# HGRN2 attention stage: first level's exponents made in the projection's last two blocks, output product's weights asked for behind the last level's products

## The reference, cut to what matters

```python
def hgrn2_chunk_scan(q, k, v, log_f):          # chunks of C = 128 tokens, two of them; 8 heads of 128
    def step(state, inp):
        qi, ki, vi, gi = inp
        b = jnp.cumsum(gi, axis=-2)
        rel = b[..., :, None, :] - b[..., None, :, :]
        decay = jnp.exp(jnp.where(lower, rel, -jnp.inf))
        attn = jnp.sum((qi[..., :, None, :] * ki[..., None, :, :]) * decay, axis=-1)
        o_intra = jnp.einsum('bhts,bhsv->bhtv', attn, vi)
        o_inter = jnp.einsum('bhtd,bhdv->bhtv', qi * jnp.exp(b), state)
        ...

def hgrn2_mixer(h, w_in, lb, norm_g, w_out):
    proj = h @ w_in                            # q, forward f, backward f, values, output gate
    ...
    o = rms_norm(o_fw + o_bw, norm_g) * jax.nn.silu(g)      # a scan forward and one backward
    return o @ w_out
```

## Time and profile before

| | us |
|---|---|
| median of 3 runs | 2471.93 (2466.46 to 2472.8) |
| the profiled execution, its own time | 2469.02 |
| its span, first to last instruction | 2467.3 |
| projection's last blocks, attention, next stage's start | 500 to 540.1, 540.1 to 608.1, from 608.1 |

### The profile page before, as it was taken

One profiled execution on the slowest core, in us unless ns is written; L12 is line 12 of the kernel. 1 busy time (PEld: TensorE's weight loads), 2 busy tenths in 40 slices (PEclk: granted clock), 3 DMA queues, 4 the chain that ended last, 5 costly groups with the idle time before them and its releaser, 6 DMA issues. The chain is left out here.

```text
span 2467.3 us, 46378 instructions
## 1 busy us (share of the span) xinstructions
PE 2294.8 (93%) x15836; PEld 1997.5 (81%) x15836; DVE 1769.4 (72%) x3162; ACT 1233.7 (50%) x1967; POOL 311.4 (13%) x289
## 2 busy tenths in 40 slices
PE   7979988987999999998999998699999999899997
PEld 7647756963699999996888887579999999788886
DVE  5764774766458887886776768466888888666776
ACT  4543543555444456554445444634446555444544
POOL 0000000000000000003443430100000000333442
PEclk9989999998999999998999999899999999999999
DMA  7554554756247776656777785234776664877775
GB/s 206 193 205 119 184 216 138 264 214 263 98 144 225 231 215 211 185 180 194 242 239 241 242 249 202 102 120 157 227 226 219 198 187 149 258 242 241 239 243 164
DMA packets 247734, 497.92 MB, mean 202 GB/s; under 512 B 58040, under 2 KB 134072, under 8 KB 244304
## 3 DMA queue, kind: packets, MB, share of 16 engines
q1 hardware_dynamic: 247632, 496.55, 62.8%
HBM read 461.82 MB, written 34.65 MB: 201 GB/s over the span
## 5 line engine op out<-in xcount | busy, mean ns | idle before, releaser
L2651 PE MATMUL psum<-split_operands 128*128 128x512 f32 x3072 | 701.0, 391 | 20.5 <-ACT split_operands L2630 20.5
L2651 PEld LDWEIGHTS psum<-split_operands 128*128 128x128 f32 x3072 | 579.3, 189 | 141.7 <-ACT split_operands L2630 20.8
L2389 PE MATMUL psum<-split_operands 128*128 128x256 f32 x4096 | 542.6, 285 | 8.9 <-ACT split_operands L2423 8.8
L2389 PEld LDWEIGHTS psum<-split_operands 128*128 128x128 f32 x4096 | 509.6, 192 | 10.4 <-ACT split_operands L2423 10.4
L2615 POOL TENSOR_TENSOR arena<-arena,residual_gates 128x256 f32 (+1 forms) x256 | 287.9, 1124 | 1644.9 <-DMA residual_gates<-expert_activations 1644.9
L2642 DVE TENSOR_TENSOR split_operands<-weights_ring,split_operands 128x1024 fp32r<-128x1024 f32 x256 | 315.3, 1232 | 201.3 <-ACT split_operands L2630 201.3
L2630 ACT CAST split_operands<-weights_ring 128x1024 fp32r<-128x1024 f32 x256 | 269.5, 1053 | 348.0 <-PE psum L2651 346.4
L2466 DVE TENSOR_TENSOR split_operands<-weights_ring,split_operands 128x1024 fp32r<-128x1024 f32 x256 | 313.1, 1224 | 101.6 <-ACT split_operands L2423 100.8
L325 PE MATMUL psum<-split_operands 128*128 128x256 f32 x2496 | 308.9, 285 | 8.0 <-DVE split_operands L341 5.5
L325 PEld LDWEIGHTS psum<-split_operands 128*128 128x128 f32 x2496 | 303.7, 193 | 15.1 <-DVE split_operands L341 8.5
L2393 PE MATMUL psum<-split_operands 128*128 128x256 f32 x2048 | 288.4, 284 | 0.0
(11 more groups left out here) (320 smaller groups left out, 2025.4 us busy)
## 6 DMA issues: line engine op xcount, KB each, us to landing
weights_ring<-in_peer_u_dram SPq DMA_DIRECT2D x256, 512.0 KB, 3.6
weights_ring<-in_peer_v_dram SPq DMA_DIRECT2D x256, 512.0 KB, 4.3
expert_activations<-residual_gates SPq DMA_DIRECT2D x256, 128.0 KB, 1.8
residual_gates<-expert_activations SPq DMA_DIRECT2D x256, 128.0 KB, 4.0
split_words<-in_w_ada_dram SPq DMA_DIRECT2D x20, 768.0 KB, 6.6
weights_ring<-in_w_in_dram SPq DMA_DIRECT2D x6, 2048.0 KB, 8.5
weights_ring<-in_hg_w_in_dram SPq DMA_DIRECT2D x5, 2048.0 KB, 8.2
arena<-in_hg_w_in_dram SPq DMA_DIRECT2D x5, 2048.0 KB, 8.0
```

Of the source, the lines that this page charges most:

```text
L2389: nc.tensor.matmul(K.ps[:, 4 + b, 0:SEQ], u_t[:, b, 0, k], h[:, wh, k], start=(k == 0 and wh == 0), stop=False)
L2651: return K.nc.tensor.matmul(K.ps[:, 4 + 2 * t + half], g[:, s, w, t * P:(t + 1) * P], vs[:, s % 2, wv, half * 512:(half + 1) * 512], start ...
```

## The change

Unit 0's exponents leave the attention stage. The buffers are now laid out in `hg_memory`, at the same addresses, and the four instructions are issued by VectorE in the projection, one at each of four places behind `FACTORS`. The counts of the semaphores `exps_k` and `exps_q` fall by one, and ScalarE waits for nothing ahead of its first exponential. The helper `level_exponent` holds what `exponents` held. SP's wait ahead of the output product's weights is now for the products of all eight units (`scored`).

```diff
+FIRST_EXPONENTS = [(8, 5), (8, 7), (9, 1), (9, 3)]
+FACTOR_BUFFERS = 3
...
+def level_exponent(K, H, pair, L, i):
+    def halves(a):
+        return a.rearrange("p n (b s j) -> p n b s j", s=2, j=L)
+
+    kf, kb = (H.k[:, d].rearrange("p h c t -> p (h c) t") for d in range(2))
+    ek, eq = (halves(pair[:, w].rearrange("p (n t) -> p n t", t=P)) for w in range(2))
+    middle_f, middle_b = (halves(H.pre[:, d, :, 0:P])[:, :, :, 1, 0:1].broadcast_to([P, HG * CH, P // (2 * L), L])
+                          for d in range(2))
+    out, a, b, op = (
+        (ek[:, :, :, 0], middle_f, halves(kf)[:, :, :, 0], ALU.add),
+        (ek[:, :, :, 1], halves(kb)[:, :, :, 1], middle_b, ALU.subtract),
+        (eq[:, :, :, 1], halves(H.pre[:, 0, :, 1:])[:, :, :, 1], middle_f, ALU.subtract),
+        (eq[:, :, :, 0], middle_b, halves(H.pre[:, 1, :, 0:P])[:, :, :, 0], ALU.subtract))[i]
+    return K.nc.vector.tensor_tensor(out, a, b, op)
...
+        elif (n, k) in FIRST_EXPONENTS:
+            i = FIRST_EXPONENTS.index((n, k))
+            level_exponent(self.K, H, H.factors[:, 0], UNITS[0], i)
...
+    H.factors = area.take(FACTOR_BUFFERS, 2, HG * CH * P)
+    H.factors_end = area.at
...
-            exponents(0)
             for n in range(NU):
                 if n + 1 < NU:
                     exponents(n + 1)
...
         @block.sync
         def _(sp):
             mod.load(sp, 2, 16)
-            sp.wait_ge(exps_q, NU)
+            sp.wait_ge(scored, NU)
...
             for n, L in enumerate(UNITS):
-                act.wait_ge(exps_k, n + 1)
+                if n >= 1:
+                    act.wait_ge(exps_k, n)
...
-                act.wait_ge(exps_q, n + 1)
+                if n >= 1:
+                    act.wait_ge(exps_q, n)
```

More of the change, by code:

```diff
@@ L1491, in stage_hg_attention @@
     nc = K.nc
-    BUFS = 3
+    BUFS = FACTOR_BUFFERS
     NU = len(UNITS)
     with S.open() as (block, sem):
-        area = Area(K.arena, H.end)
-        kq = area.take(BUFS, 2, HG * CH * P)
+        kq = H.factors
+        area = Area(K.arena, H.factors_end)
         exps_k, exps_q, exp_done, pair_ready = sem("exps_k"), sem("exps_q"), sem("exp_done"), sem("pair_ready")
@@ L1501, in stage_hg_attention @@
         q = H.q.rearrange("p h c t -> p (h c) t")
-        kf, kb = (H.k[:, d].rearrange("p h c t -> p (h c) t") for d in range(2))
-        pf, pb = H.pre[:, 0], H.pre[:, 1]
         pre = H.pre.rearrange("p d (h c) t -> p d h c t", c=CH)
@@ L1511, in crossing @@
             return kq[:, n % BUFS, w].rearrange("p (h c t) -> p h c t", h=HG, c=CH)
[L1513 to L1518, removed]
         def last_sum(d):
@@ L1538, in exponents @@
                     return
[L1539 to L1546, removed]
+                level_exponent(K, H, kq[:, n % BUFS], L, 0)
+                level_exponent(K, H, kq[:, n % BUFS], L, 1).then_inc(exps_k, 1)
+                level_exponent(K, H, kq[:, n % BUFS], L, 2)
+                level_exponent(K, H, kq[:, n % BUFS], L, 3).then_inc(exps_q, 1)
             def factors(n):
```

## The result

The changed kernel takes 2474.56 us (median of 17 runs, 2469.68 to 2478.33), the kernel before 2471.01 in as many (2466.46 to 2476.5). The ratio is 1.0013, with a 95% interval of 1.0007 to 1.0019: 3.5 us slower, between 1.7 and 4.7. It moved the way that was forecast, and by less: the forecast was 6.4. It is also less than the 0.3% that the prediction takes as the least change it can tell.

A forecast was written before the change was run, and what follows sets the result against it. VectorE paced most of the attention stage, TensorE's instruction supply its end. Terms 0 + 4.3 + 2.1 = 6.4 us over 2469.02 gave 2475.4, forecast as a 2476.5 median; range 2469.5 to 2483, 8 in 10.

The forecast's parts named there:

- Part 1: First exponents moved from attention to projection: VectorE's list 4.0 us earlier in attention, 0 us added in the projection.
- Rival C: Projection: the four added VectorE instructions aren't covered, 4.6 us on top of the forecast, 2480; chance 0.03.
- T: End of the last unit's products in attention, when the 4 MB of weights are requested: 598.5, between 594.1 and 600.3.
- rival A: Attention, TensorE: instruction lots arrive in time without bulk transfer, stops vanish, T = 594.1, 2472 as a median; chance 0.16.
- B: Attention, TensorE: instruction lots come no faster than before, T = 600.3, +8.7 us, 2479 as a median; chance 0.26.
- The end of the stage: Attention's end: SP's landing is last, next stage begins at T + 13.9 = 612.4 against 608.1, 4.3 us later.
- Rival D: Attention's end: the stores land without waiting for the weights, TensorE ends the stage, 2462 to 2465; chance 0.06.
- The clock: Next stage's first 24 TensorE records: low clock after 10.2 us idle costs 1.4 to 2.6 us more, 2.1 taken.
- the forecast (+3 to +7.4): Whole kernel: the band around the forecast of 6.4 us slower, given chance 0.46.
- Part 2: SP's request for 4 MB of weights moved from 589.47 to T, with four stores and their landing queued behind it.

The follow-up runs named there:

- part 1 alone: Changed kernel with SP's wait for the output product's weights put back to the last query exponents, first exponents still in the projection: ratio 0.9982 to before.
- part 2 alone: Kernel before with only SP's wait ahead of the weights changed to the last products, all exponents in the attention stage: ratio 1.0033 to before.
- stores first: Changed kernel with the stores of the modulation's row issued and waited for ahead of the 4 MB of weights: ratio 0.9971 to before.

## Why the prediction was right, and where a size was off

**Part 1** went as told: the first product of factors was predicted 5.1 us into the stage, and is there at 5.0. In the projection nothing was lost: the stage takes 169.3 in after and 168.2 in before, but 168.2 in part 1 alone and 169.3 in part 2 alone, so the difference isn't the added work's. Rival C falls.

**T** is the term that was mis-sized. I put the last products at 598.5, which is 58.35 from the stage's start, and they ended at 54.85: the first lot of instructions was there 2.1 us sooner (3.2 us behind unit 6's 15th record, where I had taken 5.2), and the second came 3.8 us after the first, where I had again taken 5.2. I had read 5.2 off the stop at 566.16 as the nearest row without the 4 MB, but there the modulation's weights were in transfer. Without a bulk transfer (a DMA share of 0.02) a lot takes 3.6 to 3.8 us, in the six kernels that show both stops, the changed one among them; with the 4 MB 6.3, in two. The packet of instructions itself shows what the transfer adds. In the changed kernel it is transferred at 597.7, 1.2 us behind the first record of the lot before, and TensorE goes on 2.6 us later. This is the DMA in 597.7 to 597.9:

```profile
q8 instruction: 1, 0.02, 41.6%
```

In the kernel before it is transferred at 601.5, 3.8 us behind that record (597.72), and TensorE goes on 2.5 us later (604.02). So the weights hold up the packet's start, and not what follows it. That answers rivals A and B, which stood on either side: the time of a lot is partly its own (A is wrong, 2.2 us of stop remain, though its T of 54.0 was nearer than mine) and partly the transfer's (B is wrong). The Trainium skill, "Runtime: NRT & Kernel Launch", section on instruction fetch mechanics, has the crossing mostly hidden. Here it isn't even on a quiet DMA: 127 records pass in 1.54 us, and a stop of 2.17 follows.

**The end of the stage** followed T as forecast: SP was last, 13.7 us from request to branch (13.3 forecast), the stores behind the weights. Rival D had the stores land apart from them. It falls by SP's wait of 11.4 us, which is 6.7 with half of the weights ahead and 0.9 with none, and by stores first. The stage grew by 1.2 and not by 4.3: T took off 3.5, and the landing added 0.4.

**The clock** had the right mechanism: L1725's 24 records took 7.39 in place of 5.70, 1.7 us more (2.1 forecast). Of the 3.5 to 5.9 us at the low clock that I took, 5.9 stands in a row and 3.5 in none; 4.1 were measured. What I had not counted is the second low stretch at the output product, which costs 1.7 (8 records in 5.37 us and not 3.67; the row at 628.16 shows the first 4 of them). It isn't shown to come from the change: the kernel with the weights in the next stage has it too, behind 0.74 us of idle time at the stage's start. 1.15 + 1.69 + 1.70 = 4.5 is what the two stages of the profiled executions differ by, and it lies at the upper end of what the runs show, 1.7 to 4.7.

Some of the forecast's closeness is luck. T was 3.5 us too late, and the second low stretch, which the sum didn't have, gave 1.7 back. Nor does the time alone tell the forecast (+3 to +7.4) from rival A, whose 2472 was 1.9 above the runs then known: both agree with 1.7 to 4.7. What decides is the trace: T, the stop of 2.17 us that remained, and SP as the last to arrive.

The change as a whole is two edits of opposite sign. Part 1 gives 4 us of the stage. Part 2 relieves TensorE, as its 2.2 us of stop in place of 4.6 show, and takes more by putting 4 MB ahead of four stores of 2 KB for which a whole stage waits.

## What to carry to other kernels

When a bulk load is moved later in a queue, look at what stands behind it in the same queue, and whether a stage's end waits for that: it pays the load's whole transfer, 13.7 us here for 4 MB and 8.4 for 2. Put the small stores and loads ahead of the bulk one, or the bulk one behind the meeting: with either, the kernel gained 10 to 12 us on the one before, in place of losing 3.5. And price an engine's late arrival with the low clock that follows the idle time, 2.0 us on the 24 records here.

## What the runs showed of the hardware

- Small float32 matmuls can outrun TensorE's supply of instructions: a lot of 128 records was there each 3.6 to 3.8 us at a DMA share of 0.02 and each 6.3 with 4 MB in transfer, while TensorE needed 1.54 us for 127 of them. The transfer delayed the start of the packet of instructions, from 1.2 to 3.8 us.
- Useless work can pay for itself: 24 unused matmuls in 12.6 us of waiting took the 24 records behind it from 7.39 to 5.42 us, and the kernel was some 3.5 us faster by the ratios, whose intervals meet. How much of the rest lies at stretches of low clock that fall elsewhere from kernel to kernel, whatever the idle time, these runs don't tell.
- A load of 4 KB asked for behind 4 MB landed 12.5 us after its request, and held up VectorE until then.
